# A 4-byte tile moved from ahead of two activation buffers to behind the tables: hhi and hlo start 32 bytes lower

## What is computed

```python
# first block
mod = silu(c) @ w_ada + b_ada                      # 1024 x 6144
h = rms_norm(x, norm1_w) * (1 + scale1) + shift1
q, k, v, xBC, z, dt, gates = split(h @ w_in)       # attention, state-space mixer, gates
merged = sig(gates_a) * (attn @ w_attn_out) + sig(gates_s) * (ssd @ w_ssd_out)
x = x + gate1 * (merged @ w_o)
h2 = rms_norm(x, norm2_w) * (1 + scale2) + shift2
x = x + gate2 * (square(relu(h2 @ w_mlp1)) @ w_mlp2)
# second block
u = rms_norm(x, norm1_w_2)
dq, dk, dv, sq, sk, sv = split(u @ w_in_2)         # two kinds of attention
x = x + concat(y_diff, y_sb) @ w_out_2
u2 = rms_norm(x, norm2_w_2)
x = x + (silu(u2 @ w_gate) * (u2 @ w_up)) @ w_down
```

## Time and profile before

| | us |
|---|---|
| median of 3 runs (987.2 to 991.1) | 987.58 |
| the profiled execution | 995.58 |
| its span, first to last instruction | 993.8 |
| TensorE busy in it | 924.3 |
| VectorE busy | 667.2 |
| ScalarE busy | 511.4 |

### The profile page before, as it was taken

How to read it: one execution, slowest core, us unless ns; L and a number is a source line. 1 busy time by engine, 2 the same in 40 slices (tenths; PEclk the granted TensorE clock), 3 DMA queues, 4 the chain that set the end, 5 groups by cost and what they waited for, 6 DMA issues and landing times.

```text
span 993.8 us, 18347 instructions
## 1 busy us (share of the span) xinstructions
PE 924.3 (93%) x7516; PEld 889.7 (90%) x7516; DVE 667.2 (67%) x945; ACT 511.4 (51%) x696; POOL 105.8 (11%) x85
## 2 busy tenths in 40 slices
PE   4299999899987978998999999999998999999998
PEld 4299999788866868998999999989998989999998
DVE  5855799988489998776966644453776655555542
ACT  2355654666677566343645434344568554444431
POOL 0500155300134443000000000000000000000000
PEclk9999999999999899998999999988999989999999
DMA  9755354566411224565755555535241335555550
GB/s 352 260 201 204 112 182 161 213 219 218 171 59 70 85 86 171 188 251 196 240 205 183 198 184 199 169 127 192 87 169 44 127 120 179 183 197 173 208 191 22
DMA packets 25086, 168.81 MB, mean 170 GB/s; under 512 B 2868, under 2 KB 4532, under 8 KB 4920
## 3 DMA queue, kind: packets, MB, share of 16 engines
q1 hardware_dynamic: 23616, 164.64, 47.7%
q10 hardware_dynamic: 1400, 3.16, 0.8%
HBM read 166.73 MB, written 1.06 MB: 169 GB/s over the span
## 4 chain that ended last, share of the span: by engine, by line
PE 77%; DVE 9%; ACT 7%; issue 4%; POOL 2%; DMA 1%; POOLq 0%; SPq 0%; DVEq 0%; ACTq 0%
PE bank L1689 76%; ACT kw__113 L747 2%; DVE acc L1043 2%; DMA raw<-w_stream 1%; POOL sqs L467 1%; DVE wlo L1020 1%; ACT whi L532 1%; PE bank L1872 1%; DVE kw__113 L1292 1%; DVE cvt L1185 1%; DVE eb L1283 1%; DVE hlo L1126 0%; DVE yt L1313 0%; DVE kw__113 L1299 0%; ACT zt L772 0%
## 5 line engine op out<-in xcount | busy, mean ns | idle before, releaser
L1689 PE MATMUL bank<-hhi,whi 128*128 128x256 f32 (+1 forms) x1384 | 399.5, 289 | 11.7 <-DVE hlo L1126 7.0
L1020 DVE TENSOR_TENSOR wlo<-raw,whi 128x2048 fp32r<-128x2048 f32 (+1 forms) x131 | 300.6, 2295 | 157.5 <-ACT whi L532 157.4
L1689 PE MATMUL bank<-hlo,whi 128*128 128x256 f32 (+1 forms) x1384 | 391.4, 283 | 0.0
L1689 PE MATMUL bank<-hhi,wlo 128*128 128x256 f32 (+1 forms) x1384 | 391.3, 283 | 0.0
L532 ACT ACTIVATE whi<-raw 128x2048 fp32r<-128x2048 f32 (+1 forms) x132 | 250.4, 1897 | 92.5 <-PE bank L1689 64.3
L1689 PEld LDWEIGHTS bank<-hhi,whi 128*128 128x128 f32 (+1 forms) x1384 | 265.0, 191 | 19.9 <-issue 18.2
L1689 PEld LDWEIGHTS bank<-hlo,whi 128*128 128x128 f32 (+1 forms) x1384 | 267.9, 194 | 0.3
L1689 PEld LDWEIGHTS bank<-hhi,wlo 128*128 128x128 f32 (+1 forms) x1384 | 265.2, 192 | 0.0
L1689 PE MATMUL bank<-fhi,whi 128*128 128x256 f32 x432 | 121.4, 281 | 0.0
L1689 PE MATMUL bank<-fhi,wlo 128*128 128x256 f32 x432 | 120.8, 280 | 0.0
L1689 PE MATMUL bank<-flo,whi 128*128 128x256 f32 x432 | 120.8, 280 | 0.0
(11 more groups left out here) (274 smaller groups left out, 1290.5 us busy)
## 6 DMA issues: line engine op xcount, KB each, us to landing
raw<-w_stream SPq DMA_DIRECT2D x156, 1024.0 KB, 4.9
xres<-x_t ACTq DMA_DIRECT2D x1, 1024.0 KB, 10.0
out<-oute SPq DMA_DIRECT2D x8, 128.0 KB, 4.1
tabs<-tabs_in_dram ACTq DMA_DIRECT2D x1, 641.0 KB, 5.9
tabs<-tabs_in_dram ACTq DMA_DIRECT2D x1, 512.0 KB, 3.4
hankel<-bucket_rows ACTq DMA_DIRECT2D x1, 512.0 KB, 5.6
cols<-cols_in_dram ACTq DMA_DIRECT2D x1, 325.0 KB, 12.8
tabs<-tabs_in_dram ACTq DMA_DIRECT2D x1, 64.0 KB, 12.5
```

Of the source, the lines that this page charges most:

```text
L1020: nc.vector.tensor_tensor(out=wlo[:, c % RING, 0:n], in0=raw[:, r % RING, 0:n], in1=whi[:, c % RING, 0:n].bitcast(f32), op=ALU.subtract)\
L1689: return nc.tensor.matmul(out, lhsT, rhs, start=start, stop=stop)
```

## The change

`onec` is placed behind `tabs` instead of ahead of `hhi`. By the same working as above, `hhi` now begins at 75296, `hlo` at 83488, `xres` at 91680 and `cols` at 99872, each 32 over a multiple of 64; `tabs` at 102528, `csr` at 104064 and `st` 32 bytes lower as well are now multiples of 64; `onec` is at 108192. Every tile behind it stays where it was, and so do all ahead of it, the weights among them. No instruction is added, removed or moved on any engine: only addresses differ.

```diff
     epsc = place("epsc", [P, 1], f32)
-    onec = place("onec", [P, 1], f32)
     hhi = place("hhi", [P, KD, T], f32r)
     hlo = place("hlo", [P, KD, T], f32r)
     xres = place("xres", [P, KD, T], f32)
     cols = place("cols", [P, NCOL], f32)
     tabs0 = here[0]
     tabs = place("tabs", [P, NTAB], f32)
+    onec = place("onec", [P, 1], f32)
     dtk = place("dtk", [P, NT, 2 * NH], f32)
```

## The result

The changed kernel took 1001.24 us (median of 4 runs, 998.24 to 1003.83) against 987.39 us (4 runs, 986.51 to 991.1): ratio 1.012, 95% interval 1.0089 to 1.0151, so 9 to 15 us slower. The time lies in the forecast's wide range (979 to 1009), 2 us outside its own range (990 to 999), and the loss of 13.9 us is a little over twice the 6.5 us of the sum.

What follows compares the result with a forecast made beforehand. TensorE was taken to bound the kernel. Term (a), +6.5 us, with (b) and (c) at zero, was added to the median of 987.6 us for 994 us; own range 990 to 999, wide range 979 to 1009.

Steps and rivals of the forecast that it cites:

- The bottleneck: Whole kernel: TensorE bounds it, busy 924.3 us of a span of 993.8, with 77% of the chain that ended last.
- Two rhythms that switch only at an interruption: Large matmuls run at 113.4 or 117.8 ns; what goes between decides which, and it stays until the next interruption.
- Term (a): 4,152 matmuls on hhi and hlo, streaming 32 bytes off the weights' 64-byte grid: +6.5 us, between 8.1 less and 29 more.
- The row on bd: Stream of bd beside csr's load, 32 bytes off: 393 against 391 ns, scaled to 8.3 us, 7.1 on the path.
- the other estimate: The slow rhythm, 117.8 ns, everywhere in the products on hhi and hlo: together 6.0 us more.
- (b): xres and cols go off the grid, tabs, csr and st onto it: zero, within 0.2 us either way.
- (c): onec moves, read by one-column matmuls of 100 ns each; its place doesn't enter: zero.
- Nothing changes: Large matmuls: timing sets the rhythm, the address doesn't enter; 987.6 us, 984 to 991; chance 0.22.
- Faster: The slow rhythm goes, 1,845 matmuls on hhi and hlo fall to 113.4 ns: -8.1 us, 979.5; chance 0.13.
- third rhythm: Products on hhi and hlo slow to 120 to 123 ns: 14 to 26 us more, 1002 to 1014; chance 0.14.
- The rule weighed against it: Two independent SBUF read ports, for stream and weight load: no relative address matters, the time stays 987.6 us.

## Why the prediction came out as it did

**The bottleneck: right.** TensorE alone grew, and no new wait came. Waits of VectorE and ScalarE moved by 1 or 2 us.

**Two rhythms that switch only at an interruption: right, and incomplete.** TensorE alone shows both at the same distance (448: 117.8 and 113.3). What I didn't see is that the choice also differs between executions of one program, so that what stands ahead doesn't settle it. The products on fhi in m2 show it: in both traces of the kernel before, stretches of 96 alternated between 113.3 and 117.8; in the changed kernel they all ran at 117.8, behind the same instructions and with only the address of onec changed in them.

**Term (a), a loss over the products on hhi and hlo: right in place and sign.** hhi and hlo cost (1.0103); xres, cols and tabs nothing (0.9977). The pace taken, 117.8, was near to the measured means: 117.8 ns up to m1 and 118.5 from in2 to gu. It isn't the slow rhythm, though: hhi ran with uneven steps at one of two other paces, 117.3 (m1) or 118.7 (gu in the first trace; 117.3 in the second).

**The term that was too small is (a), by the way the difference was put on the median.** The sum was made in a trace of 995.58 us, with 1,845 products of hhi and hlo slow already; 327 x 3 = 981 of them are gu's, and the second trace of the same kernel has them at 113.4. The second trace took 988.8 us, near to the median of 987.4, the first 995.6. I saw the 8 us between the two and left them unexplained, and so counted the 981 as having nothing to lose. With them, the term grows by 981 x 4.4 ns = 4.3 us, and by 0.7 ns x 1,056 = 0.7 us for gu's pace of 118.5: 6.0 + 5.0 = 11.0, 998.4 us. Measured was 1001.2 and, on another chip, 1000.3 (10.0 over its kernel before). With gu at the 117.3 of the second trace the same sum gives 9.8. The last 3 us of the first measurement it doesn't explain, unless m2's 1 to 2 us are part of them; its four executions spread over 5.6 us. From trace to trace the terms hold: before to after, the products' paces give 2.5 ns x 2,300 + 1.5 ns x 1,650 + 1.1 ns x 760 - 4.4 ns x 527 = 6.8 us of TensorE's time (hhi up to m1, hhi from in2 on, m2, dn), and the span grew by 4.1; from the second trace before, 2.4 x 2,300 + 4.6 x 1,650 + 1.7 x 760 = 14.4 us, and the span grew by 10.9. Six to eight tenths of it reach the end; I had taken three quarters for most.

**The row on bd gave a near number for a wrong reason.** It was to fall from 393 ns once csr was on the grid. After the change, window 264.7 to 265.2 us:

```profile
L1689 PE MATMUL bank<-bd,grp 128*128 128x512 f32 x2 | 0.6, 396 | 0.0
L1689 PE MATMUL bank<-bd,ngsel 128*128 128x512 f32 x1 | 0.4, 397 | 0.0
L1689 PE MATMUL bank<-ind,csr 128*128 128x512 f32 x1 | 0.4, 377 | 0.0
```

It rose to 397, and the streams beside the load of grp, whose two addresses did not change, from 391 to 396. Over the whole traces, all eight streams of bd beside a load of grp stood at 390 ns in the first trace before; in the three traces with csr and st moved (the changed kernel twice, and the kernel with only the others moved) seven, seven and six of the eight stood at 397, and with only hhi and hlo moved one did. So a pair that keeps its addresses grew longer when its neighbours moved; how stays open. "On or off the grid" was too coarse a scale for a distance that counts modulo 256, and 2 ns from one row were no measure: the 391 was the mean of 390 beside the load of grp and 392 beside another. That +8.3 us agreed with the other estimate was chance, and I leaned on the agreement.

**Terms (b) and (c), nothing:** (b) was right, by the kernel with the others alone moved. For (c), onec, the time isn't settled, as no kernel moved it alone; that its place doesn't enter is in doubt, by the stretches of m2 above. The reason given, 100 ns for each one-column matmul, looked at the length of the interruption alone and not at the rhythm behind it.

**The rivals.** *Nothing changes* fell: the rhythms do depend on timing, as it said, but on the distance too. *Faster* fell for these 32 bytes, yet its idea, that some distance lets load and stream pass each other, holds for 112 bytes, where 6 us were to be had. The *third rhythm* came true in kind, at 117.3 and 118.7 ns and not at 120 to 123; the full 120.0 belongs to other distances (0).

**The rule weighed against it.** By the Trainium skill, "TensorE: Matmul & The Clock Gate", "Step-by-step: what each phase is for", stream and load have read ports of their own. The measurements differ: TensorE alone, with nothing else at work, goes from 113.3 to 123.3 ns by address only, and moving both operands together by 32 bytes changes nothing, so two ports don't keep the two reads from hindering each other. The lines of 16 bytes that the Trainium skill gives ("SBUF — State Buffer", "Specifications (TRN2)") fit that 4 bytes (123.3) are worse than 0 (120.0), but not that 8 are as good as 0, and not that multiples of 16 differ by 7 ns.

## What to carry to other kernels

Where TensorE bounds a kernel and each weight block serves only 256 columns, take the pace of its matmuls from counts over windows, and compare it between stages: levels that differ by a few per cent at full clock, on equal instructions, can be two rhythms at one address, or come from how the two operands lie to each other. Keep the distance from weight block to moving operand under control (here modulo 256) and the place of the weight blocks with it (the gain at 112 came with them at multiples of 64), and look at it again after any edit that shifts a tile, however small. And before a difference is added to a median, find out whether the traced execution is like the ones that make the median; where they are 8 us apart, a second trace is worth more than a finer sum.

## What the runs showed of the hardware

- The pace of a 128x128 weight block with a stream of 256 columns, at a granted clock of 1.00 and TensorE alone, depends on the distance between the operands: 113.3 ns (112, 368 bytes) to 123.3 ns (4 bytes), 9%.
- At one distance (448) two stable rhythms exist, 113.3 and 117.8 ns; at another (416) three, 117.3, 118.7 and 120.0. One-column matmuls between two runs can switch from one to the other, and an undisturbed run of 1,566 products kept its own to the end.
- Moving both operands by 32 bytes makes no measurable change (ratio 0.9993, 0.9969 to 1.0017). At equal distance, weights 16 bytes over a multiple of 64 with streams on it gave 120.0 ns, and weights on it with streams 48 over gave 113.3.
- What in the memory makes this pattern stays open; no run here shows its banks or lines.
